# Joined stages, border semaphores and products that start beside the tail before them, in a fused forward pass of two transformer blocks

## The reference

```python
for l in range(DEPTH):                     # DEPTH = 2
    xn = rms_norm(h, norm_g[l])
    (a_q, a_k, a_v, i_q, i_k, i_w, b_cq, b_ckv, b_kr, c_q, c_k, c_v,
     d_u, d_v, e_q, gates, merge) = jnp.split(xn @ w_in[l], offsets, axis=-1)
    branches = (
        dsa_branch(...),     # attention on the 256 best keys
        mla_branch(...), diff_branch(...),
        sgu_branch(d_u, d_v, sgu_ln_g[l], sgu_ln_b[l], sgu_w[l], sgu_b[l]),
        memory_branch(e_q, mem_n, mem_w_kv[l]),    # attention over 256 memory tokens
    )
    mixed = functools.reduce(jnp.add, [
        jax.nn.sigmoid(merge[:, :, n]) * ((o * jax.nn.silu(gates[:, :, n])) @ w_branch[l, n])
        for n, o in enumerate(branches)])
    h = h + mixed @ w_out[l]
```

```python
def sgu_branch(u, v, ln_g, ln_b, w_s, b_s):
    vc = layer_norm(v, ln_g, ln_b).reshape(B, nc, SGU_CHUNK, SGU_GROUPS, SGU_WIDTH // SGU_GROUPS)
    w_causal = w_s * jnp.tril(jnp.ones((SGU_CHUNK, SGU_CHUNK), w_s.dtype))
    z = jnp.einsum('gij,bcjgd->bcigd', w_causal, vc) + b_s.T[None, None, :, :, None]
    return u * z.reshape(B, S, SGU_WIDTH)
```

## Time and profile before

| | us |
|---|---|
| median of 3 executions | 4938.85 (4930.86 to 4943.21) |
| the profiled execution | 4925.06 |
| its span | 4923.3 |
| TensorE busy in it | 4244.1 (86%) |
| DVE, ACT, POOL busy | 1788.9, 1465.9, 1383.4 |

### The profile page before, as it was taken

How to read it: one execution, slowest core, us unless ns; L and a number is a source line. 1 busy time by engine, 2 the same in 40 slices (tenths; PEclk the granted TensorE clock), 3 DMA queues, 4 the chain that set the end, 5 groups by cost and what they waited for, 6 DMA issues and landing times. The chain is left out here.

```text
span 4923.3 us, 60349 instructions
## 1 busy us (share of the span) xinstructions
PE 4244.1 (86%) x24494; PEld 3657.3 (74%) x24494; DVE 1788.9 (36%) x3651; ACT 1465.9 (30%) x2338; POOL 1383.4 (28%) x475
## 2 busy tenths in 40 slices
PE   6898979779879897977979789999998888868988
PEld 6677767667767676766769778888887787866766
DVE  3824343324282434332421363210114465642111
ACT  2324242223233423222322363211113343332221
POOL 1121313232212131323212221122222454532333
PEclk7798999889879899988979899999998888879999
DMA  2131313333113131333311210112221101102232
GB/s 88 31 100 39 113 50 108 97 102 101 54 40 96 44 107 48 116 91 101 100 60 52 68 24 23 48 56 61 59 60 41 39 26 39 31 18 67 75 86 73
DMA packets 484566, 323.76 MB, mean 66 GB/s; under 512 B 31729, under 2 KB 480580, under 8 KB 484292
## 3 DMA queue, kind: packets, MB, share of 16 engines
q1 hardware_dynamic: 434372, 269.57, 19.1%
q10 hardware_dynamic: 49920, 50.33, 3.1%
HBM read 316.13 MB, written 2.16 MB: 65 GB/s over the span
## 5 line engine op out<-in xcount | busy, mean ns | idle before, releaser
L70 POOL TENSOR_TENSOR w_lo<-w_raw,w_hi 128x2048 fp32r<-128x2048 f32 (+5 forms) x284 | 1128.0, 3973 | 3165.9 <-ACT w_hi L195 3165.6
L195 ACT ACTIVATE w_hi<-w_raw 128x2048 fp32r<-128x2048 f32 (+5 forms) x284 | 473.2, 1666 | 1759.2 <-PE psum L237 1759.2
L235 PE MATMUL psum<-xF_hi,w_hi 128*128 128x512 f32 x1232 | 497.2, 404 | 37.5 <-PEq L112 35.0
L237 PE MATMUL psum<-xF_hi,w_lo 128*128 128x512 f32 x1232 | 487.5, 396 | 0.0
L236 PE MATMUL psum<-xF_lo,w_hi 128*128 128x512 f32 x1232 | 484.2, 393 | 0.0
L235 PE MATMUL psum<-ffn_h_hi,w_hi 128*128 128x512 f32 (+1 forms) x1056 | 382.1, 362 | 41.7 <-POOL w_lo L70 19.5
L236 PE MATMUL psum<-ffn_h_lo,w_hi 128*128 128x512 f32 (+1 forms) x1056 | 379.4, 359 | 0.0
L237 PE MATMUL psum<-ffn_h_hi,w_lo 128*128 128x512 f32 (+1 forms) x1056 | 379.4, 359 | 0.0
L235 PE MATMUL psum<-w_hi,xF_hi 128*128 128x256 f32 (+2 forms) x960 | 275.9, 287 | 40.8 <-PEq L112 29.8
L235 PEld LDWEIGHTS psum<-xF_hi,w_hi 128*128 128x128 f32 x1232 | 234.8, 191 | 90.7 <-issue 41.6
L237 PE MATMUL psum<-w_hi,xF_lo 128*128 128x256 f32 (+2 forms) x960 | 275.0, 287 | 0.0
(11 more groups left out here) (522 smaller groups left out, 9070.2 us busy)
## 6 DMA issues: line engine op xcount, KB each, us to landing
w_raw<-in_w_in_dram SPq DMA_DIRECT2D x54, 1024.0 KB, 5.3
ada_w<-in_ada_w_dram ACTq DMA_DIRECT2D x48, 1024.0 KB, 5.0
w_raw<-in_ffn_w_in_dram SPq DMA_DIRECT2D x88, 512.0 KB, 5.1
w_raw<-in_w_in_dram SPq DMA_DIRECT2D x82, 512.0 KB, 4.2
w_raw<-in_ffn_w_out_dram SPq DMA_DIRECT2D x32, 704.0 KB, 4.6
w_raw<-in_w_branch_dram SPq DMA_DIRECT2D x80, 256.0 KB, 4.5
w_raw<-in_hg_w_in_dram SPq DMA_DIRECT2D x40, 512.0 KB, 4.0
w_raw<-in_na_w_qkv_dram SPq DMA_DIRECT2D x12, 1024.0 KB, 5.1
```

What stands on the lines that cost most here:

```text
L70: return eng.tensor_tensor(pair.lo, src, pair.hi.bitcast(F32), ALU.subtract)
L195: act.activation(self.w(j).hi, self.raw_w(j), ACT.Copy).then_inc(self.high_done, 1)
L235: pe.matmul(out, left.hi, right.hi, start=first, stop=False)
L237: return pe.matmul(out, left.lo, right.hi, start=False, stop=last)
```

## The change

- **One open block.** `stage` opens a block only if none is open and leaves it open. Each stage writes down its `ends`, semaphores with the values at which its results are there and its banks free; in the next stage each engine's program first waits for them (`enter`). Weight splits and loads are in no `ends`. Only `flush` and the end close the block; TensorE's program has 74 block borders before and 9 in the change: those of `flush`, which still come when semaphores run out, in layer 0 after the tail of dsa and after the tail of diff, between the layers, in layer 1 after the norm of diff, in the second model after the norm of the context, between the halves of the first ffn, between scan heads 2 and 3 and after the last, and the end.
- **Products that start beside the tail.** With `after_tail=True`, TensorE doesn't wait for the tail's `ends`, but for `mixed_done` 6 before unit 0, the modulation blocks before unit 2 and `mixed_done` 8 before unit 4; `first_bank=4` puts units 0 and 1 into banks 4 and 5. The diff, gating and memory branches use it. In the memory branch the norm of the memory tokens moves behind unit 1 (`norm_at=2`).
- **The tail.** `oF` and `gg` are gone: banks are multiplied in place by `sg`. The sigmoid of A waits for A alone (`merge_in`) and stands ahead of the weight split.
- **`products` on ACT** looks for due splits at every unit.
- **The gating unit** is one run of 26 units: V (8), weight transposes (2), U (8), mixes (8), with the V weights ahead of the U weights. The bias is added by ACT (`shift`), the product with U made by DVE from SBUF (`gate`). The parameters are loaded at the start, ahead of weights on SP. The last job of weights is given up by the last mix.
- **`Halves`** in `project_add` takes the place of `split_tensor`: the first four blocks run together, k by k, each k waiting for its low part.

The diff, cut to its core:

```diff
         sems = [self.sem(n) for n in names]
-        with self.nc.Block() as block:
-            yield (block, *sems)
-    def flush(self, keep=()):
-        kept = [s for s in self.spent if any(s is k for k in keep)]
-        self.nc.clear_and_free_semaphores([s for s in self.spent if not any(s is k for k in keep)])
+        if self.block is None:
+            self.opened = ExitStack()
+            self.block = self.opened.enter_context(self.nc.Block())
+        self.before, self.ends = self.ends, None
+        yield (self.block, *sems)
+        assert self.ends is not None
+    def enter(self, eng):
+        for sem, value in self.before:
+            eng.wait_ge(sem, value)
+    def close(self):
+        if self.block is not None:
+            self.opened.close()
+        self.opened, self.block, self.ends, self.after_tail = None, None, [], None
...
 def products(C, units, dve_also=None, wide=False, norms=(), wave=0, nb=None, act_also=None, pe_also=None,
-             pool_also=None, act_after=None, dve_after=None, after_norm=None):
+             pool_also=None, act_after=None, dve_after=None, norm_at=0, after_norm=None, sp_also=None, after_tail=False,
+             first_bank=0, also_ends=()):
...
-    place = C.pair if wide else C.bank
+    slot = C.pair if wide else C.bank
+    place = lambda n: slot((n + first_bank) % nb)
...
+        if sp_also:
+            block.sync(sp_also)
...
+            admit = C.after_tail if after_tail else None
+            if admit is None:
+                C.enter(pe)
...
+                if admit is not None:
+                    admit(pe, n)
+                if norm_at and n == norm_at:
+                    norms[0].pe(pe)
...
             C.high_parts(act, base)
+            C.enter(act)
             for norm in norms:
                 norm.act(act)
-            for n in by_act:
+            for n in range(len(units)):
+                if n not in by_act:
+                    C.high_parts(act, base + n + 1)
+                    continue
                 act.wait_ge(C.mm, base + n + 1)
...
+        C.ends = [(C.mm, base + len(units)), (act_took, len(by_act)), *([(dve_took, len(by_dve))] if by_dve else []), *also_ends]
...
+class Halves:
+    WAVE = 4
+    def __init__(self, C, src, pair):
+        self.src, self.pair = src, pair
+        self.high, self.low = C.sem("high"), C.sem("low")
+    def pe(self, pe):
+        pass
+    def ready(self, pe, k):
+        pe.wait_ge(self.low, k + 1)
+    def act(self, act):
+        for k in range(self.src.shape[1]):
+            act.activation(self.pair[:, k, :].hi, self.src[:, k, :], ACT.Copy).then_inc(self.high, 1)
+    def dve(self, dve):
+        for k in range(self.src.shape[1]):
+            dve.wait_ge(self.high, k + 1)
+            low_part(dve, self.pair[:, k, :], self.src[:, k, :]).then_inc(self.low, 1)
...
                     A, B = C.bank(2 * (fb % 3)), C.bank(2 * (fb % 3) + 1)
-                    if fb < 2:
-                        pe.wait_ge(o_ready, 2 * fb + 2)
-                    elif fb == 2:
-                        pe.wait_ge(gated, 2)
-                    else:
+                    if fb == 0:
+                        pe.wait_ge(low, 1)
+                    if fb >= 3:
                         pe.wait_ge(mixed_done, fb - 2)
                     C.await_w(pe, jm[fb])
-                    mm_feat(pe, A, C.w(jm[fb]), 0, C.xF, SEQ, KD)
+                    mm_feat(pe, A, C.w(jm[fb]), 0, C.xF, SEQ, KD).then_inc(merge_in, 1)
...
+                def high_part(fb):
+                    act.wait_ge(gated, fb + 1)
+                    act.activation(og[:, fb, :].hi, C.bank(fb), ACT.Copy).then_inc(high, 1)
...
                     if fb:
-                        act.wait_ge(gated, fb)
-                        act.activation(og[:, fb - 1, :].hi, oF[:, fb - 1, :], ACT.Copy).then_inc(high, 1)
-                act.wait_ge(gated, 4)
-                act.activation(og[:, 3, :].hi, oF[:, 3, :], ACT.Copy).then_inc(high, 1)
+                        high_part(fb - 1)
+                high_part(3)
                 for fb in range(8):
-                    act.wait_ge(C.mm, base + 4 + fb + 1)
-                    C.high_parts(act, base + 4 + fb + 1)
...
+                    act.wait_ge(merge_in, fb + 1)
+                    C.high_parts(act, base + 4 + fb)
                     if fb >= 2:
                         act.wait_ge(mixed_done, fb - 1)
                     act.activation(sg[:, fb % 2, :], C.bank(2 * (fb % 3)), ACT.Sigmoid).then_inc(merge_sig, 1)
+                    act.wait_ge(C.mm, base + 4 + fb + 1)
+                    C.high_parts(act, base + 4 + fb + 1)
...
+                def low_of(fb):
+                    dve.wait_ge(high, fb + 1)
+                    low_part(dve, og[:, fb, :], C.bank(fb)).then_inc(low, 1)
                 for fb in range(4):
                     dve.wait_ge(gate_sig, fb + 1)
-                    step(dve.tensor_tensor(gg[:, fb % 2, :], C.bank(4 + fb), sg[:, fb % 2, :], ALU.mult))
-                    dve.wait_ge(o_ready, fb + 1)
-                    dve.tensor_tensor(oF[:, fb, :], oF[:, fb, :], gg[:, fb % 2, :], ALU.mult).then_inc(gated, 1)
+                    dve.tensor_tensor(sg[:, fb % 2, :], C.bank(4 + fb), sg[:, fb % 2, :], ALU.mult).then_inc(gate_done, 1)
+                    dve.wait_ge(gate_done, fb + 1)
+                    dve.wait_ge(turned, fb + 1)
+                    dve.tensor_tensor(C.bank(fb), C.bank(fb), sg[:, fb % 2, :], ALU.mult).then_inc(gated, 1)
                     if fb:
-                        dve.wait_ge(high, fb)
-                        low_part(dve, og[:, fb - 1, :], oF[:, fb - 1, :]).then_inc(low, 1)
-                dve.wait_ge(high, 4)
-                low_part(dve, og[:, 3, :], oF[:, 3, :]).then_inc(low, 1)
+                        low_of(fb - 1)
+                low_of(3)
...
+                    dve.wait_ge(C.mm, base + 4 + fb + 1)
                     if n == 0:
                         dve.tensor_tensor(mixed[:, fb, :], B, sg[:, fb % 2, :], ALU.mult).then_inc(mixed_done, 1)
                     else:
-                        step(dve.tensor_tensor(gg[:, fb % 2, :], B, sg[:, fb % 2, :], ALU.mult))
-                        dve.tensor_tensor(mixed[:, fb, :], mixed[:, fb, :], gg[:, fb % 2, :],
-                                          ALU.add).then_inc(mixed_done, 1)
+                        dve.tensor_tensor(B, B, sg[:, fb % 2, :], ALU.mult).then_inc(merged, 1)
+                        dve.wait_ge(merged, fb + 1)
+                        dve.tensor_tensor(mixed[:, fb, :], mixed[:, fb, :], B, ALU.add).then_inc(mixed_done, 1)
+            C.ends = [(C.mm, base + 12), (ada_copied, NM), (ada_added, NM), (mixed_done, 8)]
+            def admit(pe, n):
+                if n == 0:
+                    pe.wait_ge(mixed_done, 6)
+                if n == 2:
+                    pe.wait_ge(ada_added, NM)
+                if n == 4:
+                    pe.wait_ge(mixed_done, 8)
+            C.after_tail = admit
...
-    jobs += in_pieces(w_in, O_DU, 1024) + tail(3)
+    jobs += in_pieces(w_in, O_DV, 512) + in_pieces(w_in, O_DU, 512) + tail(3)
...
-            products(C, [u for dst in (Q, K, V) for u in tok_units(C, C.xF, KD, dst, 512)])
+            products(C, [u for dst in (Q, K, V) for u in tok_units(C, C.xF, KD, dst, 512)], after_tail=True, first_bank=4)
...
+        def load(sp):
+            C.enter(sp)
...
+        def by_dve(u):
+            dst = V[:, u[0], u[1]:u[1] + 256]
+            return (*u[2][0:2], None, dve_copy(dst))
+        def by_act(u):
+            dst = U[:, u[0], u[1]:u[1] + 256]
+            return (*u[2][0:2], act_copy(dst), None)
+        at = [(m, c0) for c0 in (0, 256) for m in range(TT)]
+        v_units = [by_dve((*x, u)) for x, u in zip(at, tok_units(C, C.xF, KD, V, 512))]
+        u_units = [by_act((*x, u)) for x, u in zip(at, tok_units(C, C.xF, KD, U, 512))]
...
+                if g == 0:
+                    pe.wait_ge(normed, 1)
+                return pe.matmul(rows(out), wsT[:, g, :], V[:, :, c], start=True, stop=True)
+            def shift(act, out):
+                return act.activation(o[:, :, c], rows(out), ACT.Identity, bias=bs[:, g:g + 1])
+            def gate(dve, out):
+                return dve.tensor_tensor(o[:, :, c], o[:, :, c], U[:, :, c], ALU.mult)
+            return go, shift, gate
+        jv, ju = v_units[-1][0], u_units[-1][0]
+        units = v_units + [(jv, *turn(q)) for q in range(2)] + u_units + [(ju, *mix(g)) for g in range(8)]
+        def act_after(act, n):
+            if n == 12:
                 act.wait_ge(variances, 1)
                 act.activation(ru[:, :], mv[:, :, 1], ACT.Sqrt, bias=C.eps5, scale=1.0).then_inc(roots, 1)
-            @block.vector
-            def _(dve):
+        def dve_after(dve, n, took):
+            if n == 9:
                 step = Chain(dve, chain)
+                dve.wait_ge(took, 10)
+                dve.wait_ge(params, 64)
...
-                for g in range(8):
```

(14 more changed lines are left out.)

286 lines of the change are left out of this document (112 added, 174 removed).

## The result

The changed kernel took 4728.96 us in the median of four executions (4726.10 to 4735.75); the kernel before beside it took 4939.83. The ratio is 0.9577, with an interval of 0.9563 to 0.9591: 4.2% or 211 us. The prediction said 4710, within 4650 to 4790. In the later runs the same kernel took 4725.88 (0.9575, 0.9554 to 0.9597).

The account below looks back on a forecast made before the run. TensorE, busy 86% of the span, was taken as the bound. 79.3 us a layer, twice 158.6, plus 12.9, 55.8 and 0.4 made 227.7 off 4925.1: 4697, at the median's level 4711, written 4710; range 4650 to 4790.

Parts of the forecast that it names:

- The reading of the borders: Ends of blocks: TensorE waits for late barriers, not data; its largest three `PEq` kinds, 232.5 us, should fall under 80.
- The rival that nothing comes of it: All joined borders: every `enter` waits as long as its barrier did, time 4925 to 4939; chance 0.02.
- the one that the weight splits come to light: Joined borders with short first products: ten show a whole 6.4 us weight split, +64, 4775; chance 0.19.
- The hold of POOL on DVE: DVE operations with two SBUF sources stand still while POOL splits a weight: 3.88 us against 0.69 with a PSUM source.
- the first rival: Rope and gating unit's gate: POOL's split doesn't hold short operations, 19 us more gain a layer, 4673; chance 0.13.
- The term 9.9 + 2.75 up to diff's rope: mla's tail to diff's rope, each layer: 9.9 us from starting products beside the tail, 2.75 from a shorter rope gap.
- The gating unit: Diff's merge to the gating unit's tail: gain of 18.0 us in layer 0 and 27.8 in layer 1.
- the memory branch: From the gating tail to the memory branch's attention: 32.0 us gained a layer, bounds 24 and 36.
- sparse tail to mla: Border from the sparse branch's tail to mla: gain of 4.5 us in layer 1, -1.0 in layer 0.
- Inside the tail: Each tail up to its first B product: 1.4 us of a 1.67 us wait gone, 7.0 a layer.
- The scan heads: Six borders between scan heads in the second block: 17.6 of 20.3 us of barrier waits gone.
- The slower rival: Long busy stretches made by joining are throttled to clock 0.50: 12 stretches of 44 us give 4975; chance 0.02.

## Why the prediction was right

**The reading of the borders.** Right, and shown: the three kinds of waits at block ends with 232.5 us (all kinds: 333.2) are gone, 21.5 and 11.4 remain at flushes, and the barriers alone are worth 153. The rival that nothing comes of it is out, and so is the one that the weight splits come to light: waits for `w_lo` fell from 55.7 to 44.6.

**The hold of POOL on DVE.** Right in both directions. Where a source moved to PSUM the operation fell to 0.69; where a joined border brought rope and gate beside a split they grew to 4.60 and 4.39; held apart they took 0.42. With that the first rival is refuted. The prediction cited the rule of an exclusive lock for the whole instruction from the Trainium skill (SBUF — State Buffer, section "SBUF: two separate sides"), and the traces agree with it for small and strided operations as well: both held operations end 0.3 us after POOL's split (647.60 and 647.32, 882.70 and 882.41).

**Tail to products.** The term 9.9 + 2.75 up to diff's rope measured 10.8: TensorE's restart is immediate, the size was a little high in its clock part. The gating unit (18.3 and 28.3 for 18.0 and 27.8), the memory branch (32.9 for 32.0), sparse tail to mla (4.9 for 4.5), `project_add` (-1.7 and -0.6 for -0.9; behind its wave TensorE waits 3.03 us for POOL, as in the earlier trace rows, not 5 to 6) came as worked out:

```profile
1192.21 0.79 PE L256 MATMUL psum<-xF_hi,w_hi 128*128 128x512 f32 x1 [3.03 <-POOL w_lo L70]
```

**Inside the tail.** 1.84 and not 1.4, since the whole wait of 1.67 went and not 1.4 of it; behind the gating unit the clock after the 7.00 us takes it back. Writing to a bank costs 0.70, the lower bound.

**What was mis-sized.** The scan heads: 17.6 in the sum, 2.4 in the first traces, 12 in the mean of eight. The step that failed is "the next head's first products read none of it": true, but the change makes them wait for `hg_out` all the same (5.1 us), and not asked was what comes last after them. The factors do, at the end of a chain on ACT, DVE and POOL; in the first traces 14.4 of the 20.3 us came back as waits, and the 6 us in one piece cost clock. The first ffn gave 5.7 for 9.3 in the first traces and 7.2 to 8.6 in the others. The neighborhood stage lost 4.4 where nothing was forecast, and loses in every trace. These terms are of the size of the whole miss, 211 us measured for 228 summed up. The mechanisms outside them held; but the attention and the scan alone move a single execution by 10 to 20 us, so that the total came as near as this is in part luck.

**The clock.** The sum counted 2.5 us for each closed gap as if that were firm. TensorE's busy time fell by 8.6, not 30 to 50 (by 20 from the second trace before to the second after, 4250.0 to 4229.9). At diff's rope a gap 4.2 us shorter brought no clock at all, at the gating unit 2. The slower rival, that long busy stretches are throttled, did not come by its mechanism at the joined borders (1.00 in the window behind the border), but the reading under it, that the clock falls "only around idle stretches", was wrong for the kernel before already: its own trace has a fall in the middle of a busy stretch, see below.

## To carry to other kernels

Before counting a barrier as gained, name what ends last in the next stage: where it is a chain of other engines, most of the barrier's time comes back there as a wait. Give DVE one source in PSUM wherever POOL works on large tiles at the same time, and hold POOL's work back over short chains of DVE with both sources in SBUF. Compare two traces mark by mark, and take several traces of both kernels before a difference of 5 to 10 us is explained.
